# Latent attention (MLA): the weighted sum of values as three products of split operands over four query tiles, the weights normalized on GpSimd

## The chip, the cores and the metric

The kernel runs on one core of a Trainium2 chip. The metric is the device time of one execution in microseconds (us). The engines are named as in the profile: PE (TensorE), DVE (VectorE), ACT (ScalarE), POOL (GpSimd), SP (SyncE, which issues weight loads). Each engine works through its own instruction list in order; lists meet at semaphores.

## The reference

Four mixers over a sequence of 1024 tokens of width 1024 follow one another: gated linear attention, dilated window attention, differential attention and MLA. Only the MLA's core is touched. For each of 8 heads:

```python
sc = (einsum('bqhd,bkhd->bhqk', qn, k_nope) + einsum('bqhr,bkr->bhqk', qp, k_pe)) * scale
p = jax.nn.softmax(sc, axis=-1)
return jnp.einsum('bhqk,bkhd->bqhd', p.astype(v.dtype), v)
```

q and k are split into a 128-wide part of the head's own and a 64-wide rotary part; v is 128 wide. There is no mask, so each head has 1024 x 1024 weights. All is float32.

## The kernel before

The phase is `mla_phase` (line 2104). Its front part projects and rotates the rotary parts of q. Then 8 heads follow, each with 8 query tiles n of 128 queries (NT = 8). Tensors lie transposed: features on partitions, tokens along the free dimension.

Large products elsewhere in the kernel are made of split operands: x is held as x_hi (rounded to the type fp32r) and x_lo = x - x_hi, and hi*hi + hi*lo + lo*hi are summed in PSUM, by matmuls of 128x512 (`project_half`, lines 132 to 134; `scores`, lines 2191 to 2196, five matmuls for each half of the keys). The weighted sum of values (`output`, line 2220) is instead made of plain float32 matmuls of 128x128, which the trace shows as two passes each.

PSUM is 4 x 1024 columns: `at` holds the scores of two tiles in turn (and the new q and k between heads), `g.pj[:, 0]` is the one bank pair into which v and p are transposed and v is projected, `g.pj[:, 1]` gathers the head's output.

The work on one tile n, engine by engine:

- PE `scores(n)`, after the exponential of tile n-2 has freed the half of `at`.
- DVE maximum along the keys (line 2347), times -SCALE (line 2349, `nm_ready`).
- ACT exponential with the row sum (line 2286) into `p[:, n % 2]`, `exps`.
- DVE reciprocal of the sum (line 2341) and the product p * 1/sum (line 2343), `p_ready`.
- PE `turn_p(n)`: 8 transposes of p into `g.pj[:, 0]` (line 2212), after ACT has emptied that bank of the tile before.
- ACT copy into `pt[:, n % 2]` (line 2297), `pt_evac`.
- PE `output(n)`: 8 matmuls (line 2220) into the tile's 128 columns, `pv_done`.

PE's order in a head is scores(0), the transposes of v, scores(1), turn_p(0), then for n = 2 to 7 scores(n), output(n-2), turn_p(n-1); at the end the three projections of the next head (18, 12 and 12 matmuls of 128x512: q, k, v) stand between output(6), turn_p(7), output(7). DVE's order for tile n is reciprocal and product of tile n-1, then maximum and scaling of tile n. ACT's order is exponential of n, copy of n-1. At the head's end ACT copies the new q_hi, k_hi and v_t, and DVE forms q_lo, k_lo (lines 2329, 2333) and multiplies the head's output into the gate (line 2355).

POOL splits one weight slot per head (`split_slot`, lines 108 and 110), which the projections at the head's end need. SP loads the slots ahead.

Of the kernel before, what the change touches and what calls it, by code (L numbers as in the profile page):

```python
# [20 lines left out]
F32 = mybir.dt.float32  # L21
F32R = mybir.dt.float32r
# [5 lines left out]
P = 128  # L28
# [2075 lines left out]
def mla_phase(nc, g):  # L2104
# [5 lines left out]
    with ExitStack() as ctx:  # L2110
        sb = lambda n, shape, dt=F32: ctx.enter_context(nc.sbuf_tensor("mla_" + n, shape, dt))
        q_hi, q_lo, k_hi, k_lo = (g.x_hi[:, j, :] for j in range(4))
        pe_both = g.x_lo
        p, pt = sb("p", [P, 2, S]), sb("p_t", [P, 2, S])
        v, v_t = sb("v", [P, NT, P]), sb("v_t", [P, S])
        swp, q_pe = p, pt
        own = (slice(0, MLA_ROPE), slice(MLA_ROPE, P))
        mx, nm, den, rd = sb("max", [P, 2]), sb("neg_max", [P, 2]), sb("den", [P, 2]), sb("rden", [P, 2])
        names = ("swapped cosined turned pe_ready pe_hi_ready hi_ready lo_ready proj_done vt_done vt_copied v_ready s_done nm_ready exps p_ready "
                 "t_done pt_evac pv_done o_taken").split()  # L2120
        m = semaphores(nc, "mla_", names)
        block = ctx.enter_context(nc.Block())
        at = g.at
# [16 lines left out]
        @block.gpsimd  # L2140
        def _(pool):
            for j in range(PAIRS):
                if j % 2 == 0:
                    split_slot(nc, pool, g, s0 + 2 + j // 2, 0)
                pool.wait_ge(m.swapped, j + 1)
                nc.gpsimd.tensor_tensor(swp[:, j % 2, :], swp[:, j % 2, :], g.sin[:, :], ALU.mult).then_inc(m.turned, 1)
            with pool.Fori(0, PAIRS) as i:
                for u in range(2):
                    split_slot(nc, pool, g, s0 + 4 + u, i * 2)

        @block.tensor
        def _(pe):
# [26 lines left out]
            def head(i, u, last):  # L2179
                h = i * 2 + u  # L2180

                def scores(n):
                    if n == 0:
                        pe.wait_ge(m.lo_ready, h + 1)
                    elif n >= 2:
                        pe.wait_ge(m.exps, h * NT + (n - 1))
                    tile = slice(n * P, (n + 1) * P)
                    for half in range(2):
                        c = cols[half]
                        dst = at[:, (n % 2) * S:(n % 2 + 1) * S][:, c]  # L2190
                        nc.tensor.matmul(dst, q_hi[:, tile], k_hi[:, c], start=True, stop=False)
                        nc.tensor.matmul(dst, q_hi[:, tile], k_lo[:, c], start=False, stop=False)
                        nc.tensor.matmul(dst, q_lo[:, tile], k_hi[:, c], start=False, stop=False)
                        q_rot = pe_both[:, h, tile]
                        nc.tensor.matmul(dst, q_rot, g.k_pe_hi[:, c], start=False, stop=False)
                        mm = nc.tensor.matmul(dst, q_rot, g.k_pe_lo[:, c], start=False, stop=True)
                    mm.then_inc(m.s_done, 1)

                def turn_v():
                    pe.wait_ge(m.vt_copied, h + 1)  # L2200
                    for t in range(NT):
                        mm = nc.tensor.transpose(v_bank[:, t * P:(t + 1) * P], v_t[:, t * P:(t + 1) * P], g.ident[:, :])
                    mm.then_inc(m.vt_done, 1)

                def turn_p(n):
                    pe.wait_ge(m.p_ready, h * NT + (n + 1))
                    if n == 0:
                        pe.wait_ge(m.v_ready, h + 1)
                    else:
                        pe.wait_ge(m.pt_evac, h * NT + n)  # L2210
                    for t in range(NT):
                        mm = nc.tensor.transpose(g.pj[:, 0, t * P:(t + 1) * P], p[:, n % 2, t * P:(t + 1) * P], g.ident[:, :])
                    mm.then_inc(m.t_done, 1)

                def output(n):
                    pe.wait_ge(m.pt_evac, h * NT + (n + 1))
                    if n == 0:
                        pe.wait_ge(m.o_taken, h + 1)
                    for t in range(NT):
                        mm = nc.tensor.matmul(out[:, n * P:(n + 1) * P], v[:, t, :], pt[:, n % 2, t * P:(t + 1) * P],  # L2220
                                              start=(t == 0), stop=(t == NT - 1))
                    mm.then_inc(m.pv_done, 1)

                scores(0)
                turn_v()
                scores(1)
                turn_p(0)
                for n in range(2, NT):
                    scores(n)
                    output(n - 2)  # L2230
                    turn_p(n - 1)
                if not last:
                    pe.wait_ge(g.w_ready, h + (s0 + 4))
                    pe.wait_ge(m.exps, h * NT + (NT - 1))
                    project_q(1 - u)
                output(NT - 2)
                turn_p(NT - 1)
                if not last:
                    pe.wait_ge(m.exps, h * NT + NT)
                    project_k(1 - u)  # L2240
                output(NT - 1)
                if not last:
                    project_v(1 - u)

# [4 lines left out]
        def _(act):  # L2249
# [27 lines left out]

            def head(i, u, last):
                h = i * 2 + u
                for n in range(NT + 1):  # L2280
                    if n < NT:
                        b = n % 2
                        if n >= 2:
                            act.wait_ge(m.t_done, h * NT + (n - 1))
                        act.wait_ge(m.nm_ready, h * NT + (n + 1))
                        nc.scalar.activation(p[:, b, :], at[:, b * S:(b + 1) * S], ACT.Exp, bias=nm[:, b:b + 1],
                                             scale=SCALE, accum_out=den[:, b:b + 1]).then_inc(m.exps, 1)
                        if n == 0:
                            act.wait_ge(m.vt_done, h + 1)
                            nc.scalar.copy(v[:, :, :].rearrange("p t d -> p (t d)"), v_bank).then_inc(m.v_ready, 1)  # L2290
                    elif not last:
                        take_q(h + 1)
                    if n >= 1:
                        act.wait_ge(m.t_done, h * NT + n)
                        if n >= 3:
                            act.wait_ge(m.pv_done, h * NT + (n - 2))
                        nc.scalar.copy(pt[:, (n - 1) % 2, :], g.pj[:, 0, :]).then_inc(m.pt_evac, 1)
                if not last:
                    take_kv(h + 1)

# [5 lines left out]
        def _(dve):  # L2306
# [27 lines left out]

            def head(i, u, last):
                h = i * 2 + u
                for n in range(NT + 1):
                    if n >= 1:
                        b = (n - 1) % 2
                        dve.wait_ge(m.exps, h * NT + n)  # L2340
                        nc.vector.reciprocal(rd[:, b:b + 1], den[:, b:b + 1])
                        dve.drain()
                        nc.vector.tensor_scalar(p[:, b, :], p[:, b, :], rd[:, b:b + 1], None, ALU.mult).then_inc(m.p_ready, 1)
                    if n < NT:
                        b = n % 2
                        dve.wait_ge(m.s_done, h * NT + (n + 1))
                        nc.vector.tensor_reduce(mx[:, b:b + 1], at[:, b * S:(b + 1) * S], AX.X, ALU.max)
                        dve.drain()
                        nc.vector.tensor_scalar(nm[:, b:b + 1], mx[:, b:b + 1], -SCALE, None, ALU.mult).then_inc(m.nm_ready, 1)
                if not last:  # L2350
                    lower_q(h + 1)
                    lower_k(h + 1)
                dve.wait_ge(m.pv_done, h * NT + NT)
                o_h = g.o_t[:, bass.ds(h, 1), :].rearrange("p o s -> p (o s)")
                nc.vector.tensor_tensor(o_h, o_h, out, ALU.mult).then_inc(m.o_taken, 1)
                dve.drain()
# [197 lines left out]
```

## Time and profile before

| what | value |
|---|---|
| median of 3 runs | 3047.07 us (3046.64 to 3048.09) |
| profiled execution | 3045.38 us, its span 3043.6 us |
| busy in the span | PE 2818.4, DVE 1496.6, ACT 1185.8, POOL 952.7 us |
| MLA heads, first score matmul to last gate product | 2524.8 to 2931.1 us |
| granted TensorE clock over the run | 0.965 of full |

The heads are some 406 us of the span. A start time in a timeline row is in microseconds from the span's start. "xN" is the number of instructions merged in the row; a bracket gives how long the engine sat idle before it and what ended that.

### The profile page before, as it was taken

The page shows a single profiled execution, that of the slowest core. Times are in us where ns is not written, and L with a number is a line of the kernel's source. Part 1 is how long each engine was busy: PE and PEld are TensorE (multiplying, and loading weights), DVE is VectorE, ACT ScalarE, POOL GpSimd, SP SyncE. Part 2 cuts the span into 40 slices and gives each one's busy share as a digit, 9 for nine tenths or more (in the row PEclk, how much of TensorE's full clock was granted, in tenths as well). Part 3 has the DMA queues.
Part 4 walks back from the last instruction along what each step waited for, and adds up shares of the span by engine and source line. Part 5 has one row for each costly group of instructions (what it writes and reads, how often), then busy time and mean ns, then how long its engine had stood idle before and what let it go on. Part 6 is the DMA issues. An engine that isn't in the chain of part 4 may idle for free. (4 is left out here: it accounts for less than half of the span.)

```text
span 3043.6 us, 38799 instructions
## 1 busy us (share of the span) xinstructions
PE 2818.4 (93%) x14702; PEld 2310.1 (76%) x14702; DVE 1496.6 (49%) x1968; ACT 1185.8 (39%) x1974; POOL 952.7 (31%) x490
## 2 busy tenths in 40 slices
PE   7999997899999999979799999999699989999988
PEld 5887785688888888766477777777476768888876
DVE  6765565704444144555455655666533325444443
ACT  4123222424444144433445455555523324434432
POOL 3463352154334543331233232333031341000020
PEclk9999998899999999989799999999899999999999
DMA  4224323111000110021111111111041110000021
GB/s 155 89 76 131 117 70 117 70 42 42 28 28 29 42 36 28 28 95 65 58 42 42 28 43 33 37 42 35 8 152 35 42 48 15 8 14 8 9 89 56
DMA packets 57305, 162.33 MB, mean 53 GB/s; under 512 B 8400, under 2 KB 10064, under 8 KB 57168
## 3 DMA queue, kind: packets, MB, share of 16 engines
q1 hardware_dynamic: 49968, 134.17, 13.7%
q10 hardware_dynamic: 7200, 26.22, 2.7%
q8 instruction: 99, 1.62, 0.2%
q14 instruction: 38, 0.31, 0.0%
HBM read 133.99 MB, written 17.99 MB: 50 GB/s over the span
## 5 line engine op out<-in xcount | busy, mean ns | idle before, releaser
L108 POOL TENSOR_SCALAR w_hi<-w_raw 128x1024 fp32r<-128x1024 f32 x126 | 139.2, 1105 | 1499.2 <-PE pj L134 525.0
L110 POOL TENSOR_TENSOR w_lo<-w_raw,w_hi 128x1024 fp32r<-128x1024 f32 x126 | 309.2, 2454 | 19.0 <-issue 5.2
L1257 PE MATMUL pj<-x_hi,w_hi 128*128 128x512 f32 x688 | 285.5, 415 | 4.9 <-ACT swa_swapped L1388 4.9
L1259 PE MATMUL pj<-x_hi,w_lo 128*128 128x512 f32 x688 | 270.9, 394 | 0.0
L1258 PE MATMUL pj<-x_lo,w_hi 128*128 128x512 f32 x688 | 270.3, 393 | 0.0
L132 PE MATMUL pj<-x_hi,w_hi 128*128 128x512 f32 x544 | 220.0, 404 | 11.5 <-DVE gate_cumsum L550 7.5
L1708 PE MATMUL pj<-x_hi,w_hi 128*128 128x512 f32 x496 | 216.8, 437 | 7.1 <-ACT da_raw L1823 7.1
L134 PE MATMUL pj<-x_hi,w_lo 128*128 128x512 f32 x544 | 213.6, 393 | 0.0
L133 PE MATMUL pj<-x_lo,w_hi 128*128 128x512 f32 x544 | 213.4, 392 | 0.0
L1710 PE MATMUL pj<-x_hi,w_lo 128*128 128x512 f32 x496 | 196.2, 396 | 0.0
L1709 PE MATMUL pj<-x_lo,w_hi 128*128 128x512 f32 x496 | 195.3, 394 | 0.0
L1939 DVE TENSOR_REDUCE da_neg_max<-at 128x1 f32<-128x1024 f32 x128 | 150.5, 1217 | 90.3 <-PE at L1736 90.1
L1257 PEld LDWEIGHTS pj<-x_hi,w_hi 128*128 128x128 f32 x688 | 131.0, 190 | 32.4 <-issue 7.8
L1424 ACT ACTIVATE swa_p<-swa_p,swa_neg_max 128x256 f32<-128x256 f32 (+1 forms) x192 | 89.1, 465 | 170.4 <-DVE swa_neg_max L1527 170.4
L782 PE MATMUL pj<-x_hi,out_w_hi 128*128 128x512 f32 x384 | 153.0, 399 | 0.0
L1259 PEld LDWEIGHTS pj<-x_hi,w_lo 128*128 128x128 f32 x688 | 130.1, 189 | 28.7
L783 PE MATMUL pj<-x_lo,out_w_hi 128*128 128x512 f32 x384 | 150.3, 391 | 0.0
L784 PE MATMUL pj<-x_hi,out_w_lo 128*128 128x512 f32 x384 | 150.0, 391 | 0.0
L1258 PEld LDWEIGHTS pj<-x_lo,w_hi 128*128 128x128 f32 x688 | 130.4, 189 | 25.3
L782 PE MATMUL pj<-x_hi,w_hi 128*128 128x512 f32 x176 | 86.6, 492 | 61.4 <-DVE x_lo L929 34.3
L1845 ACT COPY da_p_t<-pj 128x512 f32<-128x512 f32 x128 | 74.9, 585 | 172.8 <-PE pj L1744 168.6
L1754 PEld LDWEIGHTS pj<-da_p_t,da_v 128*128 128x128 f32 x1024 | 129.6, 200 | 14.9 <-ACT da_p_t L1845 10.1
(352 smaller groups left out, 6597.3 us busy)
## 6 DMA issues: line engine op xcount, KB each, us to landing
w_raw<-w_slots SPq DMA_DIRECT2D x158, 512.0 KB, 3.5
o_t<-ada_t ACTq DMA_DIRECT2D x24, 512.0 KB, 3.5
ada_row<-ada_t ACTq DMA_DIRECT2D x24, 512.0 KB, 3.5
x_res<-o_t SPq DMA_DIRECT2D x24, 512.0 KB, 2.7
o_t<-x_res SPq DMA_DIRECT2D x24, 512.0 KB, 6.7
da_swapped<-da_raw SPq DMA_DIRECT2D x64, 128.0 KB, 2.3
o_t<-x_t SPq DMA_DIRECT2D x4, 1024.0 KB, 9.1
o_t<-x_t SPq DMA_DIRECT2D x8, 512.0 KB, 6.8
```

The costliest lines, as they stand in the source:

```text
L110: nc.gpsimd.tensor_tensor(g.w_lo[:, u, :], g.w_raw[:, u, :], g.w_hi[:, u, :], ALU.subtract)\
L132: nc.tensor.matmul(dst, w_hi, x_hi[:, k, cols], start=(j == 0), stop=False)
L133: nc.tensor.matmul(dst, w_hi, x_lo[:, k, cols], start=False, stop=False)
L134: mm = nc.tensor.matmul(dst, w_lo, x_hi[:, k, cols], start=False, stop=(j == n - 1))
L782: nc.tensor.matmul(dst, w_hi[:, w], g.x_hi[:, k, cols[half]], start=(k == 0), stop=False)
L1257: nc.tensor.matmul(proj(half), g.w_hi[:, u, w], g.x_hi[:, k, cols[half]], start=(k == 0), stop=False)
L1258: nc.tensor.matmul(proj(half), g.w_hi[:, u, w], g.x_lo[:, k, cols[half]], start=False, stop=False)
L1259: mm = nc.tensor.matmul(proj(half), g.w_lo[:, u, w], g.x_hi[:, k, cols[half]], start=False, stop=(k == KT - 1))
L1708: nc.tensor.matmul(proj(half), g.w_hi[:, u, w], g.x_hi[:, k, cols[half]], start=(k == 0), stop=False)
L1709: nc.tensor.matmul(proj(half), g.w_hi[:, u, w], g.x_lo[:, k, cols[half]], start=False, stop=False)
L1710: mm = nc.tensor.matmul(proj(half), g.w_lo[:, u, w], g.x_hi[:, k, cols[half]], start=False, stop=(k == KT - 1))
L1939: nc.vector.tensor_reduce(nm[:, col:col + 1], map_banks(c), AX.X, ALU.max, negate=True).then_inc(m.nm_ready, 1)
```

## The change

Four things change in the heads (and buffers with them).

1. `output` gathers four query tiles: `output(half)` makes 8 x 3 = 24 matmuls of 128x512 from split operands (v_hi*pt_hi, v_hi*pt_lo, v_lo*pt_hi), twice per head. output(0) stands between scores(6) and turn_p(4), output(1) after turn_p(7).
2. The splits that this needs: ACT writes `pt_hi` (rounded) from the transposed weights, with strided output, and DVE then forms `pt_lo` = bank - pt_hi (`lower_p`), which now frees the bank (`pt_evac`). v likewise: ACT v_hi, DVE v_lo.
3. The product p * 1/sum goes from DVE to POOL (`normalize`), in place; the head's weight split follows normalize(2) on POOL.
4. The orders: turn_p comes one tile later on PE (scores(n), turn_p(n-2)), and the ACT copy likewise (exponential n, copy n-2). DVE's order becomes reciprocal n-1, maximum n, scaling n, lower_p(n-2). p lies in the two rope tables, which are done with by then, pt_hi in free slots of x_hi, and v_t, v_hi, v_lo, pt_lo over the front part's buffers.

```diff
@@ POOL @@
-            with pool.Fori(0, PAIRS) as i:
-                for u in range(2):
-                    split_slot(nc, pool, g, s0 + 4 + u, i * 2)
+            def normalize(h, n):
+                b = n % 2
+                pool.wait_ge(m.rd_ready, h * NT + (n + 1))
+                nc.gpsimd.tensor_scalar(p[b][:, :], p[b][:, :], rd[:, b:b + 1], 0.0, ALU.mult, ALU.add).then_inc(m.p_ready, 1)
+            for h in range(MLA_HEADS):
+                for n in range(NT):
+                    normalize(h, n)
+                    if n == 2:
+                        split_slot(nc, pool, g, s0 + 4 + h % 2, h - h % 2)
@@ PE @@
-                def output(n):
-                    pe.wait_ge(m.pt_evac, h * NT + (n + 1))
-                    if n == 0:
+                def output(half):
+                    pe.wait_ge(m.pt_evac, h * NT + (4 * half + 4))
+                    if half == 0:
                         pe.wait_ge(m.o_taken, h + 1)
+                    dst = out[:, cols[half]]
                     for t in range(NT):
-                        mm = nc.tensor.matmul(out[:, n * P:(n + 1) * P], v[:, t, :], pt[:, n % 2, t * P:(t + 1) * P],
-                                              start=(t == 0), stop=(t == NT - 1))
+                        nc.tensor.matmul(dst, v_hi[:, t, :], pt_hi[:, t, :], start=(t == 0), stop=False)
+                        nc.tensor.matmul(dst, v_hi[:, t, :], pt_lo[:, t, :], start=False, stop=False)
+                        mm = nc.tensor.matmul(dst, v_lo[:, t, :], pt_hi[:, t, :], start=False, stop=(t == NT - 1))
                     mm.then_inc(m.pv_done, 1)
                 scores(1)
-                turn_p(0)
                 for n in range(2, NT):
                     scores(n)
-                    output(n - 2)
-                    turn_p(n - 1)
+                    if n == 6:
+                        output(0)
+                    turn_p(n - 2)
                 if not last:
                     project_q(1 - u)
-                output(NT - 2)
-                turn_p(NT - 1)
+                turn_p(NT - 2)
                 if not last:
                     project_k(1 - u)
-                output(NT - 1)
+                turn_p(NT - 1)
+                output(1)
@@ ACT @@
+                def take_p(n):
+                    act.wait_ge(m.t_done, h * NT + (n + 1))
+                    if n % 4 == 0:
+                        act.wait_ge(m.pv_done, h * 2 + n // 4)
+                    nc.scalar.copy(pt_hi[:, :, (n % 4) * P:(n % 4 + 1) * P], g.pj[:, 0, :].rearrange("p (t q) -> p t q", q=P)).then_inc(m.pt_high, 1)
-                for n in range(NT + 1):
+                for n in range(NT + 2):
                     if n < NT:
...
-                            nc.scalar.copy(v[:, :, :].rearrange("p t d -> p (t d)"), v_bank).then_inc(m.v_ready, 1)
-                    elif not last:
+                            nc.scalar.copy(v_hi[:, :, :].rearrange("p t d -> p (t d)"), v_bank).then_inc(m.vh_ready, 1)
+                    elif n == NT and not last:
                         take_q(h + 1)
-                    if n >= 1:
-                        act.wait_ge(m.t_done, h * NT + n)
-                        if n >= 3:
-                            act.wait_ge(m.pv_done, h * NT + (n - 2))
-                        nc.scalar.copy(pt[:, (n - 1) % 2, :], g.pj[:, 0, :]).then_inc(m.pt_evac, 1)
+                    if n >= 2:
+                        take_p(n - 2)
@@ DVE @@
+                def lower_p(n):
+                    dve.wait_ge(m.pt_high, h * NT + (n + 1))
+                    own_cols = slice((n % 4) * P, (n % 4 + 1) * P)
+                    nc.vector.tensor_tensor(pt_lo[:, :, own_cols], g.pj[:, 0, :].rearrange("p (t q) -> p t q", q=P),
+                                            pt_hi[:, :, own_cols], ALU.subtract).then_inc(m.pt_evac, 1)
-                for n in range(NT + 1):
-                    if n >= 1:
+                for n in range(NT + 2):
+                    if 1 <= n <= NT:
                         b = (n - 1) % 2
                         dve.wait_ge(m.exps, h * NT + n)
-                        nc.vector.reciprocal(rd[:, b:b + 1], den[:, b:b + 1])
-                        dve.drain()
-                        nc.vector.tensor_scalar(p[:, b, :], p[:, b, :], rd[:, b:b + 1], None, ALU.mult).then_inc(m.p_ready, 1)
+                        nc.vector.reciprocal(rd[:, b:b + 1], den[:, b:b + 1]).then_inc(m.rd_ready, 1)
+                        if n == 1:
+                            dve.wait_ge(m.vh_ready, h + 1)
+                            nc.vector.tensor_tensor(v_lo[:, :, :].rearrange("p t d -> p (t d)"), v_bank,
+                                                    v_hi[:, :, :].rearrange("p t d -> p (t d)"), ALU.subtract).then_inc(m.v_ready, 1)
                     if n < NT:
...
+                    elif n == NT and not last:
+                        lower_q(h + 1)
+                    if n >= 2:
+                        lower_p(n - 2)
                 if not last:
-                    lower_q(h + 1)
                     lower_k(h + 1)
```

## Rows read from the trace of the kernel before

**Rows 1.** The page's first part: busy us (share of span) and instructions by engine
```profile
PE 2818.4 (93%) x14702; PEld 2310.1 (76%) x14702; DVE 1496.6 (49%) x1968; ACT 1185.8 (39%) x1974; POOL 952.7 (31%) x490
```

**Rows 2.** Windows, one head: busy PE, PEld, DVE, ACT, POOL; granted clock, DMA share, GB/s
```profile
2577.50:2629.00 51.50, 50.78 (x324) 45.00 (x323) 21.75 (x35) 21.44 (x28) 3.43 (x2) 1.00 0.04 11
```

**Rows 3.** Timeline, PE, one tile: start us, us, engine line, operation
```profile
2592.58 1.95 PE L2220 MATMUL pj<-mla_p_t,mla_v 128*128 128x128 f32 x16
2594.36 1.04 PE L2212 MATMUL pj<-ident,mla_p 128*128 128x128 f32 x8
2595.16 0.48 PE L2191 MATMUL at<-x_hi 128*128 128x512 f32 x1
...
2597.52 1.95 PE L2220 MATMUL pj<-mla_p_t,mla_v 128*128 128x128 f32 x16
```

**Rows 4.** Timeline, DVE and ACT, the same tile
```profile
2597.72 1.23 DVE L2347 TENSOR_REDUCE mla_max<-at 128x1 f32<-128x1024 f32 x1 [1.22 <-PE at L2196]
2599.03 0.15 DVE L2349 TENSOR_SCALAR mla_neg_max<-mla_max 128x1 f32<-128x1 f32 x1
...
2599.21 1.11 ACT L2286 ACTIVATE mla_p<-at,mla_neg_max 128x1024 f32<-128x1024 f32 x1 [2.75 <-DVE mla_neg_max L2349]
...
2600.38 1.02 ACT L2297 COPY mla_p_t<-pj 128x1024 f32<-128x1024 f32 x1
...
2600.45 0.16 DVE L2341 RECIPROCAL mla_rden<-mla_den 128x1 f32<-128x1 f32 x1 [1.27 <-ACT mla_p L2286]
...
2600.69 0.75 DVE L2343 TENSOR_SCALAR mla_p<-mla_p,mla_rden 128x1024 f32<-128x1024 f32 x1
```

**Rows 5.** Waits in the MLA heads: us in total, times, longest us
```profile
ACT mla_p L2286 <- DVE mla_neg_max L2349: 162.5, 64, 7.9
```

**Rows 6.** Timeline, starts of the second and third head, PE and DVE
```profile
2577.75 0.39 PE L2191 MATMUL at<-x_hi 128*128 128x512 f32 x1
...
2629.01 0.39 PE L2191 MATMUL at<-x_hi 128*128 128x512 f32 x1
...
2631.28 1.04 PE L2202 MATMUL pj<-ident,mla_v_t 128*128 128x128 f32 x8
2631.48 1.22 DVE L2347 TENSOR_REDUCE mla_max<-at 128x1 f32<-128x1024 f32 x1 [3.40 <-PE at L2196]
```

**Rows 7.** Timeline, end of the second head: ACT, then the DVE that waits for it
```profile
2624.69 1.01 ACT L2274 CAST x_hi<-at 128x1024 fp32r<-128x1024 f32 x1 [1.72 <-PE at L134]
2625.73 1.22 DVE L2333 TENSOR_TENSOR x_hi<-at,x_hi 128x1024 fp32r<-128x1024 f32 x1 [4.17 <-ACT x_hi L2274]
```

**Rows 8.** One line's instructions: the transposes of v, first and last start
```profile
L2202 PE MATMUL pj<-ident,mla_v_t x64: 272/273/273, 2528.8 to 2888.3; 128*128 128x128 f32 x64
```

**Rows 9.** Timeline, end of the MLA phase: the last DVE operation
```profile
2929.91 1.22 DVE L2355 TENSOR_TENSOR o_t<-o_t,pj 128x1024 f32<-128x1024 f32 x1 [6.05 <-PE pj L2220]
```

**Rows 10.** Groups by line and shape, POOL, whole run
```profile
L110 POOL TENSOR_TENSOR w_lo<-w_raw,w_hi 128x1024 fp32r<-128x1024 f32 x126 | 309.2, 2454 | 19.0 <-issue 5.2
L108 POOL TENSOR_SCALAR w_hi<-w_raw 128x1024 fp32r<-128x1024 f32 x126 | 139.2, 1105 | 1499.2 <-PE pj L134 525.0 <-PE pj L1710 375.8 <-PE pj L1259 242.1
```

**Rows 11.** Timeline, front part of the MLA phase: DVE beside POOL
```profile
2497.46 3.38 DVE L2323 TENSOR_TENSOR mla_p_t<-mla_p_t,mla_p 128x1024 f32<-128x1024 f32 x1 [5.45 <-POOL mla_p L2146]
...
2499.73 2.02 POOL L108 TENSOR_SCALAR w_hi<-w_raw 128x1024 fp32r<-128x1024 f32 x1
2500.76 1.21 DVE L2320 TENSOR_TENSOR mla_p_t<-pj,rope_cos 128x1024 f32<-128x1024 f32 x1
```

**Rows 12.** Groups by line and shape, ACT, first block: a copy into runs of 128
```profile
L470 ACT COPY gla_v<-at 128x1024 f32<-128x1024 f32 x6 | 6.0, 1006 | 1.4 <-DVE ada_dots L600 1.4
```

**Rows 13.** Windows: tail of the differential attention
```profile
2145.00:2165.00 20.00, 14.80 (x106) 10.79 (x104) 14.37 (x20) 12.25 (x20) 0.00 (x0) 1.00 0.01 2
2165.00:2185.00 20.00, 14.78 (x77) 11.90 (x77) 11.48 (x15) 9.05 (x18) 0.00 (x0) 0.74 0.00 0
```

**Rows 14.** Timeline, PE, tail of the differential attention
```profile
2167.29 3.78 PE L1754 MATMUL pj<-da_p_t,da_v 128*128 128x128 f32 x16 [0.93 <-ACT da_p_t L1845]
```

More of the change, by code:

```diff
@@ L2113, in mla_phase @@
         pe_both = g.x_lo
-        p, pt = sb("p", [P, 2, S]), sb("p_t", [P, 2, S])
-        v, v_t = sb("v", [P, NT, P]), sb("v_t", [P, S])
-        swp, q_pe = p, pt
+        with ExitStack() as front:
+            swp, q_pe = (front.enter_context(nc.sbuf_tensor("mla_front_" + n, [P, 2, S], F32)) for n in ("swapped", "q_pe"))
+        v_t, v_hi, v_lo = sb("v_t", [P, S]), sb("v_hi", [P, NT, P], F32R), sb("v_lo", [P, NT, P], F32R)
+        pt_hi, pt_lo = g.x_hi[:, 4:8, :].rearrange("p a (b q) -> p (a b) q", q=HALF), sb("p_t_lo", [P, NT, HALF], F32R)
+        p = (g.cos, g.sin)
         own = (slice(0, MLA_ROPE), slice(MLA_ROPE, P))
         mx, nm, den, rd = sb("max", [P, 2]), sb("neg_max", [P, 2]), sb("den", [P, 2]), sb("rden", [P, 2])
-        names = ("swapped cosined turned pe_ready pe_hi_ready hi_ready lo_ready proj_done vt_done vt_copied v_ready s_done nm_ready exps p_ready "
-                 "t_done pt_evac pv_done o_taken").split()
+        names = ("swapped cosined turned pe_ready pe_hi_ready hi_ready lo_ready proj_done vt_done vt_copied vh_ready v_ready s_done nm_ready exps rd_ready p_ready "
+                 "t_done pt_high pt_evac pv_done o_taken").split()
         m = semaphores(nc, "mla_", names)
@@ L2211, in turn_p @@
                     for t in range(NT):
-                        mm = nc.tensor.transpose(g.pj[:, 0, t * P:(t + 1) * P], p[:, n % 2, t * P:(t + 1) * P], g.ident[:, :])
+                        mm = nc.tensor.transpose(g.pj[:, 0, t * P:(t + 1) * P], p[n % 2][:, t * P:(t + 1) * P], g.ident[:, :])
                     mm.then_inc(m.t_done, 1)
-                def output(n):
-                    pe.wait_ge(m.pt_evac, h * NT + (n + 1))
-                    if n == 0:
+                def output(half):
+                    pe.wait_ge(m.pt_evac, h * NT + (4 * half + 4))
+                    if half == 0:
                         pe.wait_ge(m.o_taken, h + 1)
+                    dst = out[:, cols[half]]
                     for t in range(NT):
-                        mm = nc.tensor.matmul(out[:, n * P:(n + 1) * P], v[:, t, :], pt[:, n % 2, t * P:(t + 1) * P],
-                                              start=(t == 0), stop=(t == NT - 1))
+                        nc.tensor.matmul(dst, v_hi[:, t, :], pt_hi[:, t, :], start=(t == 0), stop=False)
+                        nc.tensor.matmul(dst, v_hi[:, t, :], pt_lo[:, t, :], start=False, stop=False)
+                        mm = nc.tensor.matmul(dst, v_lo[:, t, :], pt_hi[:, t, :], start=False, stop=(t == NT - 1))
                     mm.then_inc(m.pv_done, 1)
@@ L2285, in head @@
                         act.wait_ge(m.nm_ready, h * NT + (n + 1))
-                        nc.scalar.activation(p[:, b, :], at[:, b * S:(b + 1) * S], ACT.Exp, bias=nm[:, b:b + 1],
+                        nc.scalar.activation(p[b][:, :], at[:, b * S:(b + 1) * S], ACT.Exp, bias=nm[:, b:b + 1],
                                              scale=SCALE, accum_out=den[:, b:b + 1]).then_inc(m.exps, 1)
@@ L2349, in head @@
                         nc.vector.tensor_scalar(nm[:, b:b + 1], mx[:, b:b + 1], -SCALE, None, ALU.mult).then_inc(m.nm_ready, 1)
+                    elif n == NT and not last:
+                        lower_q(h + 1)
+                    if n >= 2:
+                        lower_p(n - 2)
                 if not last:
-                    lower_q(h + 1)
                     lower_k(h + 1)
-                dve.wait_ge(m.pv_done, h * NT + NT)
+                dve.wait_ge(m.pv_done, h * 2 + 2)
                 o_h = g.o_t[:, bass.ds(h, 1), :].rearrange("p o s -> p (o s)")
```

## The prediction

> **What bounds the kernel now.** I read the page first. PE is busy for 93% of the span [rows 1], but that is a mean over many stages, so I asked for the busy time of single MLA heads. In the second head PE works 50.78 of 51.50 us at full granted clock, DVE 21.75 and ACT 21.44 [rows 2]. The heads are PE-bound, and every microsecond taken from PE there looks like a gain. The timeline of one tile shows the target: the 8 matmuls of line 2220 are 16 passes, and they occupy PE from 2592.58 to 2594.36, 1.78 us, the transposes until 2595.16, 0.80 us, and the next tile's output starts at 2597.52, so a tile takes 4.94 us with nothing idle on PE [rows 3].
>
> The next view is the same tile on DVE and ACT. Maximum starts 2597.72, scaling 2599.03 (1.31 later), exponential 2599.21 (0.18), copy 2600.38 (1.17), reciprocal 2600.45 (1.24 after the exponential's start) [rows 4]. The longest wait in total is ACT for DVE's scaling, 162.5 us in 64 times [rows 5]: it costs nothing today, because PE is never kept waiting for long. But these are engines that wait for each other, and their low busy share says nothing on how long a loop through both is.
>
> **Part 1, the products.** A group of four tiles costs 24 matmuls of 128x512. Ten such matmuls (scores(0)) run from 2629.01 to 2631.28 [rows 6], 0.227 us each, so a group is 5.46 us and a head 10.9, against 8 x 1.78 = 14.2 now: PE is relieved of 3.3 us per head, 27 us in all. I keep this apart from the result, since it counts only if PE stays the bound.
>
> **Part 2, the order of DVE and ACT.** On ACT the copy of tile n-2 stands behind the exponential of n. On DVE lower_p(n-2) waits for that copy, and the maximum of n+1 stands behind lower_p(n-2). So a loop closes with each engine waiting for the other in turn: maximum(n), scaling, exponential(n), copy(n-2), lower_p(n-2), reciprocal(n), maximum(n+1). Before, DVE's next maximum stood behind only the reciprocal and product of the tile before. The terms: 1.31 + 0.18 + 1.17 [rows 4]; from the copy's start to the subtraction that waits for it 1.04, and the subtraction 1.22 [rows 7], taken from the same pair of operations on k, also out of PSUM; reciprocal 0.16 and handing on 0.02. The loop is 5.10 us per tile. PE needs 2.27 + 0.80 = 3.07 us for scores and transposes in that time and is idle for 2 us. A tile in the middle of a head thus takes 5.1 us instead of 4.94, although its output has left it.
>
> **Part 3, what stands at the ends.** I put one head down from its first score matmul at 0. Maximum(0) starts at 2.47 (2629.01 to 2631.48) [rows 6], exponential(0) at 3.96, v_hi at 5.13, and now v_lo on DVE, new, at 6.17. Maximum(1), queued behind v_lo, starts at 7.40, exponential(1) at 8.89, reciprocal(1) at 10.13, maximum(2) at 10.30. From there the loop: maximum(3) at 15.4, (4) 20.5, (5) 25.6, and lower_p(3) from 29.30 to 30.52. Only then may output(0) start. It holds PE until 36.0, turn_p(4) is queued behind it and ends at 37.1, and exponential(6) waits for that; it was due at 30.7 + 1.49 = 32.2. The group product thus delays the loop by 4.9 us, once per head. The new wait of copy(4) for output(0) adds nothing to it, and scores(7), also queued behind, still ends at 39.2, in time. Then copy(4) 38.3, lower_p(4) 39.3 to 40.5, maximum(7) 40.7, exponential(7) 42.2, copy(5) 43.4, lower_p(5) to 45.6. turn_p(6) ends at 46.7; meanwhile project_q is done (45.7) and ACT takes q_hi. Copy(6) to 47.8, DVE's q_lo to 48.0, lower_p(6) to 49.2, turn_p(7) to 50.3, copy(7) to 51.3, lower_p(7) to 52.6. Output(1) runs to 58.1 with nothing beside it, project_v (12 matmuls, 2.7) to 60.8. A head before took 2629.01 - 2577.75 = 51.26 us [rows 6]. The difference is +9.6 us, for seven heads +67.
>
> The last head has no projections. Before, its first score matmul is at 2577.75 + 6 x 51.26 = 2885.3, which fits the last v transpose at 2888.3 [rows 8], and the last gate product starts at 2929.91 [rows 9], 44.6 later. Now the chain above gives 58.2: +13.6.
>
> **Part 4, the normalization on POOL.** The trace has no POOL product with a per-partition scalar. The nearest row is the split's first step, 1.105 us; its second, with two tensor operands, is 2.454 [rows 10]. DVE took 0.75 for the same [rows 4], which I take as the lower bound. I use 1.1, since the form is that of the first row. It hides: between reciprocal(n) and turn_p(n) lies about one loop (5 us) in the middle, and 3.5 us at the tail (45.7 to 49.2). At 2.454 it costs nothing either; above 3.5, each further microsecond costs 8 us in all. The weight split behind normalize(2), 1.1 + 2.45, delays normalize(3) to about its due time, and turn_p(3) comes 5 us later; project_q needs the slot only at the end. Taking the product from DVE saves 0.7 us per tile on DVE, already left out of the loop. Could POOL slow DVE? In the front part a DVE product with both inputs in SBUF took 3.38 us beside POOL, one with an input in PSUM 1.21 [rows 11]; every large DVE operation of the new heads reads PSUM. The Trainium skill (GPSIMD Engine Reference, its opening) calls GpSimd the wrong choice for elementwise work, with VectorE about twice as fast. The rows agree on the order (1.105 against 0.75), and by that rule the sum stays as it is, because the price is hidden.
>
> **Part 5, the strided writes.** take_p and lower_p write runs of 128 columns. An ACT copy from PSUM into runs of 128 takes 1.006 us here [rows 12], no more than a dense one; for DVE no row shows it, and I take the dense 1.22. If either took twice its time, the loop would be 1 us longer, some 56 us in all. A strided write has no less to move than a dense one, so there is no gain to bound.
>
> **Part 6, the clock.** PE now pauses for 2 us per tile. The nearest rows are the tail of the differential attention, where short bursts stand between pauses: at much the same busy time the granted clock was 1.00 for 20 us and 0.74 in the next 20 [rows 13], and 16 passes of value matmuls in that second stretch, at the 1.2 GHz level, took 3.78 us [rows 14] against 1.95 at the full clock [rows 3]. So a group product can cost 5.1 us more. In the tile loop the lower clock would fill the pause and cost little. I take it for the last head's output(1), before which PE has only three sets of transposes in 13 us, and nothing elsewhere: +4. The bounds are 0 and both products of every head.
>
> **Sum.** 67 + 13.6 + 4 = 84.6. The span 3043.6 becomes 3128.2; 1.8 us lie around it (3045.38), and the median of the runs is 1.7 above the profiled execution: 3131.7 us, rounded to 3132.
>
> **The rivals.**
> - PE stays the bound (not slower, faster). PE's own work per head is 18.2 + 6.4 + 0.8 + 10.9 + 9.5 = 45.9 us against 51.26; seven heads save 37, the last 3: 3007 us. For it: busy shares of 42% on DVE and ACT [rows 2]. Against: the loop of part 2. The case decides at that loop's length: it breaks even at about 3.5 us instead of 5.1, so 1.6 us of its five terms would have to overlap. Chance 0.06.
> - The clock falls in most heads. If output(1) and project_v run at 1.2 GHz in every head, that is about 7 x 7 us more: 3180; with output(0) too, 3215. For it: the same rows [rows 13]; against: PE makes ten dense matmuls in every loop. The Trainium skill (TensorE: Matmul & The Clock Gate, A second HAM failure mode: psum-queue depth-cycling) tells of a kernel whose clock oscillated from short idles between groups of matmuls. Chance 0.20.
> - A strided DVE or ACT operation or POOL's product is dearer than taken: about 3188. Chance 0.07.
> - The forecast's case: 0.67.
>
> **How the numbers follow.** Within the forecast's case, small DVE operations that overlap (0.2 us per loop, some 11 us), gaps at the heads' ends (10 us) and no clock loss give 3107 at the low side; partial clock loss adds 25 to 50 at the high side. The range 3100 to 3190 leaves out the first rival and the far end of the second. This kernel can be told from no change by about 0.2%, 6 us. Faster 0.06, same 0.01, slower 0.93.
>
> **What would show it.** A head of about 61 us; maxima 5.1 us apart, each starting right behind a reciprocal; PE idle for 2 us per tile until DVE's lower_p; exponential(6) 10 us behind exponential(5), waiting for transposes; output(1) alone for 5.5 us. Maxima 3.5 us apart or less would make the loop wrong; group products of 10 us would be the clock. POOL's product longer than 3.5 us would break part 4.

## The result, and the profile after

The kernel after takes 3134.34 us (median, 3130.75 to 3146.65) beside 3047.49 (3046.64 to 3048.09) for the one before: ratio 1.0292 [1.0263, 1.0322], slower. The forecast was 3132, with a range of 3100 to 3190. The profiled execution took 3130.75 us, its span is 3129.0, 85.4 more than before. Seven heads, from the copy of v_t to the copy of v_t, took 363.9 us and now take 435.7: +71.8. From the last such copy to the last gate product it was 44.4 us and is now 62.0: +17.6. Together that is 89.4; 2.3 us of it are given back ahead of the heads, whose first v_t copy is that much earlier, and the rest behind them.

The page's busy line and the windows of the second and the fourth head, in the columns of [rows 2]:

```profile
PE 2815.3 (90%) x14062; PEld 2272.9 (73%) x14062; DVE 1536.2 (49%) x1976; ACT 1181.2 (38%) x1974; POOL 1023.8 (33%) x554
```

```profile
2586.30:2648.70 62.40, 51.46 (x244) 41.34 (x243) 25.60 (x36) 20.83 (x28) 12.39 (x10) 0.95 0.03 9
2710.20:2770.40 60.20, 48.48 (x243) 38.96 (x243) 25.61 (x36) 20.84 (x28) 12.38 (x10) 1.00 0.03 9
```

PE is busy for 51.5 of 62.4 us and for 48.5 of 60.2, where it was 50.8 of 51.5 [rows 2]. DVE works more and ACT about the same; both stand idle for more than half of a head. The head grew by the time in which PE waits. The second head takes 2.2 us more than the fourth; the column PEclk, the granted clock, has 0.95 for it against 1.00, and part 6 below shows the slow rows.

One tile in the loop, the timeline of all engines (answers [rows 3, 4]):

```profile
2606.78 1.21 DVE L2376 TENSOR_REDUCE mla_max<-at 128x1 f32<-128x1024 f32 x1
...
2608.07 0.15 DVE L2378 TENSOR_SCALAR mla_neg_max<-mla_max 128x1 f32<-128x1 f32 x1
...
2608.25 1.11 ACT L2309 ACTIVATE rope_cos<-at,mla_neg_max 128x1024 f32<-128x1024 f32 x1 [2.71 <-DVE mla_neg_max L2378]
...
2609.36 1.00 ACT L2301 CAST x_hi<-pj 128x1024 fp32r<-128x1024 f32 x1
...
2610.39 1.23 DVE L2361 TENSOR_TENSOR mla_p_t_lo<-pj,x_hi 128x1024 fp32r<-128x1024 f32 x1 [2.17 <-ACT x_hi L2301]
2611.53 0.15 DVE L2368 RECIPROCAL mla_rden<-mla_den 128x1 f32<-128x1 f32 x1
2611.61 1.21 DVE L2376 TENSOR_REDUCE mla_max<-at 128x1 f32<-128x1024 f32 x1
...
2611.76 1.06 PE L2223 MATMUL pj<-ident,rope_sin 128*128 128x128 f32 x8 [1.45 <-DVE mla_p_t_lo L2361]
```

Read it from one maximum to the next: maximum 2606.78, scaling 1.29 later, exponential 0.18, the copy behind it on ACT 1.11, DVE's subtraction 1.03, reciprocal 1.14, maximum 0.08. That is 4.83 us, and the brackets close it: ACT has waited 2.71 us for the scaling, DVE 2.17 us for the copy, and PE 1.45 us for the subtraction. In the 4.81 us from 2606.95 to 2611.76, one tile on PE, DVE is busy for 2.6 us, ACT for 2.1 and PE for 3.4, and still each of them waits for the next.

The waits over all heads: who waits for whom, us in total, times, longest. The copy that DVE waits for is `take_p`, recorded as x_hi; mla_p_t_lo is the subtraction `lower_p`.

```profile
DVE mla_p_t_lo L2361 <- ACT x_hi L2301: 172.3, 57, 7.5
...
ACT rope_cos L2309 <- PE pj L2223: 64.3, 8, 8.1
...
PE pj L2223 <- DVE mla_p_t_lo L2361: 56.7, 34, 3.8
```

### The profile page after: what moved, and what is told of

It is laid out like the page before. It is cut to its first block and busy times, and to the rows that moved or that the text cites. A ratio compares the mean times of both kernels' runs of the same rounds, so it can differ in the third digit from the quotient of the medians.

```text
span 3129.0 us, 37483 instructions
## 1 busy us (share of the span) xinstructions
PE 2815.3 (90%) x14062; PEld 2272.9 (73%) x14062; DVE 1536.2 (49%) x1976; ACT 1181.2 (38%) x1974; POOL 1023.8 (33%) x554
## 5 line engine op out<-in xcount | busy, mean ns | idle before, releaser
L2361 DVE TENSOR_TENSOR mla_p_t_lo<-pj,x_hi 128x1024 fp32r<-128x1024 f32 x64 | 78.3, 1223 | 172.3 <-ACT x_hi L2301 172.3
L1258 PEld LDWEIGHTS pj<-x_lo,w_hi 128*128 128x128 f32 x688 | 130.3, 189 | 25.3
```

Of the source, the lines that this page charges most:

```text
L1258: nc.tensor.matmul(proj(half), g.w_hi[:, u, w], g.x_lo[:, k, cols[half]], start=False, stop=False)
```

## The experiments

Kernels of after have its line numbers, shifted by a few where lines were added or left out. Ratios are against the kernel before on the same chip.

**The changed kernel on another chip.**

> The changed kernel unaltered, on this chip, as the partner of the other kernels of this call: 3134 by both theories.

3138.46 us, ratio 1.0309 [1.0291, 1.0326]. It serves as the second yardstick for kernels that differ little from after.

**The loop: the copy of n-2 ahead of the exponential of n.** One edit on after, ACT's order.

```diff
                 for n in range(NT + 2):
+                    if 2 <= n < NT:
+                        take_p(n - 2)
...
-                    if n >= 2:
+                    if n >= NT:
                         take_p(n - 2)
```

> The changed kernel with one order altered: for tiles 2 to 7 ACT does the copy of tile n-2 before the exponential of tile n instead of after it. Same instructions, same PE order. Loop theory (the new heads are bound by maximum, scaling, exponential, copy, subtraction, reciprocal in turn, 4.8 us per tile in the trace): the copy no longer waits for the maximum, so the loop falls apart; next is the loop through the one transposed bank, transposes 1.06 + copy 1.04 + subtraction 1.22 = 3.3 us. A head falls from 61.5 to about 54.5 us and the time from 3134 to about 3080. Rival (the work itself is what costs: 24 product matmuls, two splits and POOL's product): the order changes nothing, 3134.

3073.82 us, ratio 1.0089 [1.0066, 1.0112]: some 70% of the loss is gone by the order of two instructions. The timeline, a tile of the second head:

```profile
2599.74 1.23 DVE L2378 TENSOR_REDUCE mla_max<-at 128x1 f32<-128x1024 f32 x1
...
2599.86 1.06 PE L2223 MATMUL pj<-ident,rope_cos 128*128 128x128 f32 x8 [0.16 <-DVE mla_p_t_lo L2363]
...
2600.96 1.01 ACT L2301 CAST x_hi<-pj 128x1024 fp32r<-128x1024 f32 x1 [1.40 <-PE pj L2223]
...
2602.01 1.22 DVE L2363 TENSOR_TENSOR mla_p_t_lo<-pj,x_hi 128x1024 fp32r<-128x1024 f32 x1 [0.81 <-ACT x_hi L2301]
...
2603.26 1.23 DVE L2378 TENSOR_REDUCE mla_max<-at 128x1 f32<-128x1024 f32 x1
...
2603.38 1.06 PE L2223 MATMUL pj<-ident,rope_sin 128*128 128x128 f32 x8 [0.15 <-DVE mla_p_t_lo L2363]
```

Maxima are 3.52 us apart instead of 4.83. What binds now is the one bank pair: transposes at 2599.86, copy 1.10 later, subtraction 1.05 later, the next transposes 1.37 later, 3.52 together, and PE waits for the subtraction before each set. DVE and ACT do the same work in both kernels; only its order on ACT differs. So the loop of part 2 is shown to be the cause of these 60 us: PE's work is the same in both kernels and can't be what they were lost to.

**The group product on the loop.** output(0) with 3 of its 24 matmuls, output(1) whole (the weighted sums of the first four query tiles are left incomplete).

```diff
+                    tiles = range(NT) if half else range(1)
-                    for t in range(NT):
+                    for t in tiles:
```

> The changed kernel with the first group product of each head cut to one key tile: output(0) makes 3 of its 24 matmuls, 4.8 us less on PE per head; the weighted sums of the first four query tiles are left incomplete. By the prediction's part 3 the group product stands wholly on the loop, with its own time less the 1.7 us that the loop's turn there would take anyway: 4.8 us less per head, 38 us in all, 3098. Rival (the products fall into PE's pauses of 2 us per tile and are hidden in good part): 15 us less or none. Less than 38 can also come from PE working less and the clock falling more often.

3095.52 us, ratio 1.0173 [1.0156, 1.0190]: 39 us less than after, 36 by the ratios. Twenty-one matmuls a head at 0.228 us are 4.8, or 38 in eight heads. In after, the group product and the engines behind it:

```profile
2616.50 0.49 PE L2233 MATMUL pj<-x_hi,mla_v_hi 128*128 128x512 f32 x1 [1.34 <-DVE mla_p_t_lo L2361]
...
2622.09 1.04 PE L2223 MATMUL pj<-ident,rope_cos 128*128 128x128 f32 x8
...
2623.25 1.12 ACT L2309 ACTIVATE rope_cos<-at,mla_neg_max 128x1024 f32<-128x1024 f32 x1 [8.06 <-PE pj L2223]
...
2625.39 1.22 DVE L2361 TENSOR_TENSOR mla_p_t_lo<-pj,x_hi 128x1024 fp32r<-128x1024 f32 x1 [7.53 <-ACT x_hi L2301]
```

and with the short product:

```profile
2613.91 0.50 PE L2234 MATMUL pj<-x_hi,mla_v_hi 128*128 128x512 f32 x1 [1.36 <-DVE mla_p_t_lo L2362]
...
2615.86 1.12 ACT L2310 ACTIVATE rope_cos<-at,mla_neg_max 128x1024 f32<-128x1024 f32 x1 [3.27 <-PE pj L2223]
```

In after the transposes of tile 4 start at 2622.09, right behind the product, and exponential(6) has waited 8.06 us for them; with the short product it waits 3.27 us, 4.8 less. Nothing of output(0) is hidden: nearly the whole of what was taken from it passes into the time. These 39 us are not to be added to the 60 of the loop: the kernel before pays for its value products too, 14.2 us a head (part 1).

**Is PE the bound?** The fifth score product (q_rot with k_pe_lo, 128 matmuls, 29 us of PE in all) is left out, once of before and once of after; the scores lose that term.

```diff
-                        nc.tensor.matmul(dst, q_rot, g.k_pe_hi[:, c], start=False, stop=False)
-                        mm = nc.tensor.matmul(dst, q_rot, g.k_pe_lo[:, c], start=False, stop=True)
+                        mm = nc.tensor.matmul(dst, q_rot, g.k_pe_hi[:, c], start=False, stop=True)
```

> The kernel before with the same 128 score matmuls left out (a low-order term of the scores). If PE is the bound of its heads, as the windows say, all 29 us appear: 3018. If the heads before were already bound by a loop through DVE and ACT, close to 3047.

> The changed kernel without the fifth score matmul (q_rot with k_pe_lo) of each half: 2 x 64 matmuls of 0.23 us less on PE, 29 us in all; this leaves a low-order term out of the scores. Loop theory: PE's work in tiles 2 to 7 stands in its pauses and is free; only scores(0) of each head stands on the path: 3 to 8 us less, about 3128. Rival (PE is still the bound and its work sets the time): 29 us less, 3105.

Of before: 3024.2 us, ratio 0.9930 [0.9903, 0.9957], about 20 us of the 29. The value products of two tiles in a row, and two of PE's waits over the heads:

```profile
2590.08 1.95 PE L2219 MATMUL pj<-mla_p_t,mla_v 128*128 128x128 f32 x16
...
2594.58 1.95 PE L2219 MATMUL pj<-mla_p_t,mla_v 128*128 128x128 f32 x16
```

```profile
PE pj L2211 <- DVE mla_p L2342: 8.5, 8, 1.1
PE pj L2219 <- ACT mla_p_t L2296: 6.7, 10, 1.1
```

A tile now takes 4.50 us instead of 4.94 [rows 3], the whole of the two matmuls. Of the other 9 us, 8 are in PE's waits for the product and the copy, which have grown from 7.2 us to 15.2. Most of them stand where a head begins, at its first transposes (1.1 us in seven of the eight heads) and at its first value product (0.57 us in each). So before was bound by PE, in its tiles fully.

Of after: 3142.14 us, ratio 1.0312 [1.0286, 1.0338], which can't be told from after (1.0292, and 1.0309 on the other chip). The same 29 us are worth 20 in one kernel and nothing in the other. The heads even look longer (443.4 us for seven, against 435.7 and 436.7), and PE's timeline shows why in output(0), which in after ran through at 0.39 us a matmul:

```profile
2621.51 0.50 PE L2232 MATMUL pj<-x_hi,mla_v_hi 128*128 128x512 f32 x1 [1.81 <-DVE mla_p_t_lo L2360]
...
2622.77 0.54 PE L2234 MATMUL pj<-x_hi,mla_v_lo 128*128 128x512 f32 x1
2623.12 0.63 PE L2232 MATMUL pj<-x_hi,mla_v_hi 128*128 128x512 f32 x1
```

Behind the sixth matmul seven take 0.63. Output(0) has such slow matmuls in four of the eight heads, this one included, each time behind a pause of 1.8 to 1.9 us where after has 1.3 to 1.4. That the missing work brought the clock down is the likeliest reading, since all four executions have a granted clock of 0.949 to 0.953, below the 0.954 to 0.960 of the nine of after; how much of the saved time the clock took is not measured.

**The clock before output(1).** Ten matmuls into columns that output(1) then overwrites, put before its wait.

```diff
                 def output(half):
+                    if half == 1:
+                        for t in range(10):
+                            nc.tensor.matmul(out[:, cols[1]], v_hi[:, 0, :], g.k_pe_hi[:, cols[1]], start=True, stop=True)
```

> The changed kernel with 10 more matmuls of 128x512 (v_hi with k_pe_hi, into the columns that output(1) overwrites) issued before PE waits for the last subtraction of a head, so PE works through the 2.4 us pause ahead of output(1). Clock theory: in five of eight heads output(1) ran in part at the 1.2 GHz level after this pause (7.0 us against 5.6); with the pause filled it runs at 2.4 GHz, and the time falls by 5 to 10 us to about 3127, although PE has 18 us more to do. Rival (the low clock has another cause, or the heads differ for another reason): no change, 3134, or up to some us more where the matmuls delay output(1).

3125.08 us, ratio 1.0263 [1.0237, 1.0289]; after on the other chip has [1.0291, 1.0326]. Seven heads take 427.6 us instead of 435.7, and, counted from the transposes of v to the next ones, each takes 60.2 to 60.7 us instead of 60.2 to 62.5. PE, second head: in after, transposes and the start of output(1),

```profile
2601.38 1.94 PE L2223 MATMUL pj<-ident,rope_sin 128*128 128x128 f32 x8 [2.52 <-DVE mla_p_t_lo L2361]
```

```profile
2638.96 0.79 PE L2233 MATMUL pj<-x_hi,mla_v_hi 128*128 128x512 f32 x1 [2.36 <-DVE mla_p_t_lo L2361]
2639.55 0.63 PE L2234 MATMUL pj<-mla_p_t_lo,mla_v_hi 128*128 128x512 f32 x1
...
2642.09 0.39 PE L2234 MATMUL pj<-mla_p_t_lo,mla_v_hi 128*128 128x512 f32 x1
```

and with the filling:

```profile
2637.39 1.06 PE L2223 MATMUL pj<-ident,rope_sin 128*128 128x128 f32 x8
2638.22 2.57 PE L2230 MATMUL pj<-mla_k_pe_hi,mla_v_hi 128*128 128x512 f32 x10
2640.82 0.50 PE L2236 MATMUL pj<-x_hi,mla_v_hi 128*128 128x512 f32 x1
2641.16 0.40 PE L2237 MATMUL pj<-mla_p_t_lo,mla_v_hi 128*128 128x512 f32 x1
```

In after, output(1) starts 2.36 us after the transposes' end, its first seven matmuls take 0.79 to 0.57 us, the 1.2 GHz level, and from 2642.09 on 0.39. With 2.57 us of filling in the same pause none of its 24 is slow, in any of the eight heads, and turn_p(1) is slow in two heads (1.35 and 1.51 us) instead of four. So 18 us more of work on PE took some 8 us from the heads. For the whole kernel the gain is small: the interval overlaps that of after itself and only just misses that of the second chip. The spans of the heads and the rows carry it.

**POOL.** First the product on POOL alone, on before; then after with a second POOL pass over the weights (times 1.0) behind a drain and ahead of the signal. The cut shows the added pass.

```diff
+                nc.gpsimd.tensor_scalar(p[b][:, :], p[b][:, :], 1.0, 0.0, ALU.mult, ALU.add).then_inc(m.p_ready, 1)
```

> The kernel before with one part of the change alone: the product p * 1/sum on POOL instead of DVE, with the weight split behind the third of a head. PE stays the bound. Between reciprocal and transposes PE has an output and scores to do, so POOL's 1.1 us instead of 0.75 shows only at a head's first tile, where PE waits already: 0 to 4 us slower, 3046 to 3050. Rival (POOL's hand-over or the weight split behind it costs on every tile): 20 us or more.

3043.68 us, ratio 1.0001 [0.9990, 1.0011]. PE waits for the product 8.1 us in all, once a head, where it waited 5.0 us for DVE's:

```profile
PE pj L2216 <- POOL mla_p L2151: 8.1, 8, 1.0
```

> The changed kernel with a second POOL product (times 1.0) behind each normalization, so that POOL takes about 2.25 us per tile instead of 1.12. Cover theory (between a reciprocal and the transposes lies a loop of 4.8 us, 3.5 at the tail): no change, 3134. Rival (POOL's product stands on the path of every tile): +1.1 us x 64 = 72 us, 3206. In between, if only the tile behind the weight split or the head's last tile is exposed: 8 to 16 us.

3134.98 us, ratio 1.0291 [1.0276, 1.0307]; the same chip has 1.0309 for after. The two groups of POOL's form, in the second kernel:

```profile
L2154 POOL TENSOR_SCALAR rope_sin<-rope_sin,mla_rden 128x1024 f32<-128x1024 f32 x32 | 36.0, 1126 | 61.4 <-DVE mla_rden L2370 59.6 <-issue 1.8
...
L2156 POOL TENSOR_SCALAR rope_sin<-rope_sin 128x1024 f32<-128x1024 f32 x32 | 33.7, 1054 | 5.2 <-issue 5.2
```

The step is 2.2 us long instead of 1.1 and costs nothing that can be measured: part 4's margin of 3.5 us is not reached.

**Towards a better version.** On the kernel with the copy first: v_lo behind maximum(1) and the transposes of v behind scores(1).

```diff
                 scores(0)
-                turn_v()
                 scores(1)
+                turn_v()
```

> The kernel with the copy first on ACT, and v taken off the head's first path: PE transposes v after scores(1) instead of before, DVE forms v_lo after maximum(1) instead of before. In the trace of the changed kernel maximum(1) comes 4.8 us after maximum(0), with v_hi and v_lo between. If the order is what costs there, about 3 us per head go, 25 us against the 3074 of the kernel with the copy first: 3047 to 3050. Rival (v's steps only move): unchanged, 3074.

3056.88 us, ratio 1.0045 [1.0030, 1.0060]. By the ratios that is 13 us less than with the copy first alone, about half of the 25 expected; a head takes 52.9 us instead of 55.1. With the filling, and q_lo behind lower_p(6):

> The kernel just named, with the 10 filling matmuls ahead of output(1) and with DVE's q_lo behind lower_p(6) instead of ahead of it (1 us per head at the tail). Clock theory: 5 to 12 us less than without, 3036 to 3043, at or just below the kernel before. Rival (the filling matmuls only cost, since a shorter pause leaves less room): equal or some us slower than without.

3053.35 us, ratio 1.0025 [1.0012, 1.0039], which can't be told from the version above: the 5 to 12 us expected are not shown, and it is still slower than before. Tiles stay at 3.52 us, the bank's loop. Then the bank is handed on in halves of four key tiles:

```diff
+                    for j in range(2):
+                        act.wait_ge(m.t_done, h * 2 * NT + (2 * n + j + 1))
...
+                        nc.scalar.copy(pt_hi[:, 4 * j:4 * j + 4, (n % 4) * P:(n % 4 + 1) * P],
+                                       g.pj[:, 0, cols[j]].rearrange("p (t q) -> p t q", q=P)).then_inc(m.pt_high, 1)
```

> On the best version so far (copy first, v late, filled pause): the transposed bank is passed on in halves of four key tiles, each with its own transposes, copy and subtraction and its own count. In the trace of that version a tile takes 3.52 us, the loop transposes, copy, subtraction through the one bank, while PE has 3.1 us of work. Bank theory: in halves the loop falls below PE's work and a tile takes about 3.1 us: 6 x 0.4 us per head, 15 to 20 us less, about 3035, below the kernel before. Rival (the fixed cost of twice as many copies and subtractions eats it; DVE then has 1.37 + 0.08 + 1.4 us per tile): no change, 3053, or slower.

3030.82 us, ratio 0.9957 [0.9941, 0.9973]: 0.4% faster than before, and the interval leaves 1 out. Its timeline:

```profile
2590.39 1.04 PE L2224 MATMUL pj<-ident,rope_cos 128*128 128x128 f32 x8
...
2591.03 1.08 ACT L2306 CAST x_hi<-pj 128x512 fp32r<-128x512 f32 x2 [0.91 <-PE pj L2224]
...
2592.01 1.29 DVE L2371 TENSOR_TENSOR mla_p_t_lo<-pj,x_hi 128x512 fp32r<-128x512 f32 x2
...
2593.57 1.03 PE L2224 MATMUL pj<-ident,rope_sin 128*128 128x128 f32 x8
...
2593.77 1.23 DVE L2382 TENSOR_REDUCE mla_max<-at 128x1 f32<-128x1024 f32 x1 [0.29 <-PE at L2207]
```

Transposes are 3.18 us apart. The copy begins 0.64 us after the first transpose instead of 1.10, and the maximum now waits for PE's scores: in its tiles the kernel is PE-bound again. A head takes 50.1 us against 52.0 before, by the seven heads of each (350.7 and 363.9). Last, turn_p(4) ahead of output(0):

> The kernel just named with turn_p(4) ahead of output(0) instead of behind it. turn_p(4) needs nothing of output(0), so the exponential of tile 6 and the chain behind it no longer stand behind 5.5 us of products; but the copy of tile 4 still waits for output(0), which reads the columns that it overwrites. If exponential(6) is what output(0) holds back: 1 us per head, 8 us less. If the copy is: no change.

3026.32 us, ratio 0.9950 [0.9936, 0.9964], not to be told from the version above; seven heads take 350.4 us against 350.7. Its trace tells which of the expectation's two cases holds. In the second head ACT waits for the end of output(0) with the copy of tile 4, which now stands ahead of exponential(6):

```profile
2599.36 1.07 ACT L2306 CAST x_hi<-pj 128x512 fp32r<-128x512 f32 x2 [6.82 <-PE pj L2239]
```

So it is the copy that output(0) holds back. Its window of 50 us, in the columns of [rows 2]:

```profile
2580.00:2630.00 50.00, 49.72 (x257) 41.75 (x258) 27.57 (x46) 21.84 (x37) 12.76 (x11) 1.00 0.03 11
```

PE works for 49.7 of 50 us at full clock, 2.5 of them in the ten filling matmuls, and the kernel is some 15 us faster than before. That the relief of part 1 pays once the loop is below PE's own time is the likely reason, but it is not shown by itself: the late transposes of v were never tried on the kernel before.

## Why the prediction was right, and where it was off

**Part 1.** output(0) took 2616.50 to 2622.09, 5.59 us, against 5.46. That PE's relief counts only if PE is the bound is what the two kernels without the fifth product show: 20 us in one, none in the other.

**Part 2.** The loop was forecast at 5.10 and is 4.83. The 0.27 lies in the small terms: the reciprocal starts 1.14 us after the start of a subtraction that lasts 1.23, the maximum 0.08 after the reciprocal instead of 0.18, the copy 1.11 behind the exponential instead of 1.17. Here an operation starts before the record of the one ahead of it on its engine ends, where it does not read its result. PE's pause in a tile, forecast at 2 us, is 1.45. The rival that PE stays the bound broke even at 3.5 us; the kernel with the copy first has just that loop, 3.52, yet is 0.9% slower, because a head is more than its loop: it still takes 55.1 us against 52.0, and moving v's steps alone gave back 2.2 of them.

**Part 3.** The second head, forecast and measured, in us from its first score matmul (2586.32): maximum(3) 15.4 and 14.9, maximum(5) 25.6 and 25.3, output(0) 30.5 and 30.2, exponential(6) 37.1 and 36.9, lower_p(6) 48.0 and 47.9, output(1) 52.6 and 52.6. This close agreement is partly luck: the second head holds a slow set of transposes that the forecast did not have (part 6), and it made up for 0.7 us of the loop's error. In the fourth head, at full clock throughout and from 2710.24, the same steps come at 14.9, 24.6, 29.4, 36.2, 47.1 and 51.9, each but the first 0.7 to 1.1 us ahead of the forecast:

```profile
2734.79 1.21 DVE L2376 TENSOR_REDUCE mla_max<-at 128x1 f32<-128x1024 f32 x1
...
2739.68 0.50 PE L2233 MATMUL pj<-x_hi,mla_v_hi 128*128 128x512 f32 x1 [1.36 <-DVE mla_p_t_lo L2361]
```

The full-clock heads (4 and 7) took 60.20 and 60.31 against the forecast 60.8. The late exponential(6) is the second row of the waits above, 64.3 us in 8 times. The last head's part, 13.6 + 4, measured 17.6.

**Parts 4 and 5.** The forms, over the heads:

```profile
L2361 DVE TENSOR_TENSOR mla_p_t_lo<-pj,x_hi 128x1024 fp32r<-128x1024 f32 x64 | 78.3, 1223 | 172.3 <-ACT x_hi L2301 172.3
...
L2301 ACT CAST x_hi<-pj 128x1024 fp32r<-128x1024 f32 x64 | 64.4, 1007 | 25.8 <-PE pj L2223 25.8
...
L2154 POOL TENSOR_SCALAR rope_cos<-rope_cos,mla_rden 128x1024 f32<-128x1024 f32 x32 | 35.9, 1122 | 294.8 <-DVE mla_rden L2368 294.8
```

POOL's product takes 1.12 us (taken: 1.1) and hides. By the Trainium skill (GPSIMD Engine Reference, its opening) VectorE would be about twice as fast; the rows say 1.12 against 0.75, 1.5 times. The strided writes take 1.22 on DVE (taken: 1.22) and 1.01 on ACT, so no stride is paid for.

**Part 6** is the term that was mis-sized. "+4 for the last head, nothing elsewhere" saw the mechanism and misplaced it. In six of the eight heads 6 to 12 of output(1)'s matmuls ran at the lower level, in the last head 12, so that it took 8.25 us there until the last gate product:

```profile
3017.01 1.22 DVE L2387 TENSOR_TENSOR o_t<-o_t,pj 128x1024 f32<-128x1024 f32 x1 [8.30 <-PE pj L2235]
```

turn_p(1) took 1.5 to 1.9 us instead of 1.06 in four heads. In the second head that is at 2601.38 after 2.52 us of idle, and made the distance of two maxima 5.56 instead of 4.83, since the next exponential waits for these transposes:

```profile
2603.43 1.11 ACT L2309 ACTIVATE rope_sin<-at,mla_neg_max 128x1024 f32<-128x1024 f32 x1 [3.46 <-PE pj L2223]
```

So part 6 was also wrong in saying that the lower clock would only fill the pause in the tile loop: here it cost 0.73 us, and output(1) 1.44 us more, together the 2.2 us between the second and the fourth head. Counted from the transposes of v to the next ones, both full-clock heads took 60.25 us on average, the five others of the first seven 61.6 to 62.5, 8.9 us more in all. The seven heads close: 7 x (60.25 - 51.26) = 62.9, plus 8.9, is the 71.8 measured, against 67 forecast. So two errors of 4 and 9 us cancelled in part, in the last head +17.6 came out because output(1) lost 2.8 us and sets of transposes at 1.94 us most of the rest, and the sum of 84.6 met 85.4 better than its terms deserved. The heads themselves lost 89.4; it is the 4.0 us given back ahead of and behind them, which no term foresaw, that bring the span's difference to 85.4. The mechanism of the forecast is right, and that its number came out within 3 us is in part luck.

The reason that failed: "PE makes ten dense matmuls in every loop", as an argument against the second rival. It held for output(0), none of whose matmuls was slow in any head, behind a pause of 1.3 to 1.4 us. It did not hold for turn_p(1), which has the ten matmuls of scores(3) right ahead of it and then a pause of 2.5 us, nor for output(1), which stands behind a set of transposes and a pause of 2.4 us. By the Trainium skill (TensorE: Matmul & The Clock Gate, A second HAM failure mode: psum-queue depth-cycling) short idles between groups can make the clock swing; the trace agrees, at 0.93 to 1.00 over the first seven heads and 0.83 in the last. So the second rival was right in kind, six of the eight heads fell, and wrong in size: 8.9 us over seven heads instead of its 49, since in each only a part of output(1) and at most one set of transposes ran at the lower level. What decides whether a given head falls stays open: heads with equal orders and equal pauses differ, and on the second chip it was the third and the sixth that kept the full clock. With its pause filled output(1) fell in no head; nothing was tried on the pause ahead of turn_p(1).

## What to carry to other kernels

A PE-bound stage with DVE and ACT at 42% is not one in which they have 58% to spare: write down the closed loop of waits through all engines, add up starts to starts, and compare it with PE's own time before giving DVE or ACT more to do per tile. A buffer that is emptied by two engines in turn (copy, then subtraction) is held for the sum of both, and here the order on ACT was worth 60 us and halves of the bank some 21. A long product put between two short steps of such a loop costs its whole length, however well its operands are cut.

## What the runs showed of the hardware that had not been expected

- Removing 29 us of matmuls did not help, and the granted clock over the run was lower without them (0.949 to 0.953, against 0.954 to 0.960 with them, on two chips). Adding 18 us of filling went with a higher one (0.960 to 0.962) and took 8 us from seven heads.
- Ten matmuls of filling kept a following product at 0.39 us each; the same product after 2.36 us of idle behind transposes began at the lower level (0.79, then 0.63) in five heads, and in one fell there from its fourth matmul on.
- DVE and ACT wrote runs of 128 columns at the price of dense writes, 1223 and 1007 ns, against 1224 (v_lo) and 1007 ns (v_hi).
- POOL's product slowed no DVE operation that reads PSUM: the maxima, which run beside it (2611.61 above, with POOL's product from 2611.78), take 1211 ns as a mean, 1223 before.
